# Expert weights in three pairs of buffers, activation rows in a ring of four, and the second gather moved to the end of GpSimd's step

## The chip, the cores and the metric

One core of one Trainium2 chip runs the whole kernel. The time is in device microseconds (us) for one execution; lower is better. Of the kernel before there are three timed runs and one profiled execution.

## The reference

One layer of a hybrid decoder for 520 tokens (512 prompt tokens and 8 new ones), width 1024, all in float32: attention and a recurrent branch side by side, a layer norm, then a mixture of experts and a second layer norm. The change touches only the last part:

```python
# 32 experts in 4 groups of 8; each token goes to the 2 best experts of its best group
for e in range(N_EXPERTS):
    gu = xt @ w_gate_up[e]                                # (n, 1024) @ (1024, 512)
    h = jax.nn.silu(gu[:, :D_EXPERT]) * gu[:, D_EXPERT:]
    y = y + gate[:, e:e + 1] * (h @ w_down[e])            # (n, 256) @ (256, 1024)
...
return _layernorm(ALPHA * x1 + ffn, ln2_g, ln2_b)
```

The weights of one expert are 3 MB (2 MB gate-up, 1 MB down), 96 MB in all. They are read from HBM once.

## The kernel before

The first part (about 340 us) computes attention, recurrence, output projection, first layer norm and the routing. The second part goes through the 32 experts in 16 pairs. A pair has 128 slots, 64 tokens for each of its two experts, and TensorE works on both experts side by side. Pair n is one *step*. Every token is in two slots, at an earlier and a later pair: the pair at which it comes first stores its expert's result in `first_rows` in HBM; the pair at which it comes second fetches that (the *partner's* rows), adds it, weighted, to its own, does the layer norm and stores the token's final row.

The order on each engine is written out by hand, with semaphores between engines. The first three pairs (HEAD) and the last five stand apart; eight (BODY) are in a loop that runs once here. In step n:

- **TensorE** (`products`, L970): gate-up product of pair n, in two halves of the weights (`gu_half`, `gu_ps`); then it turns the rows of pair n+1 (L955). Then `experts`: it waits for `h_ready` (VectorE), turns the hidden values, waits for their copy and does the down product (L993, `dn_ps`).
- **ScalarE**: silu (L1265), half of the turned rows' copy (L1253), the hidden values' copy (L1269), the copy of the down product to `yb` (L1276, `ya_done`), and `root(n-2)` (L1280) for the layer norm.
- **VectorE** (`pair_step`): `hidden(n)` (L1923, signals `h_ready`), `tokens_out(n+1)` (L1856), `residual(n+1)` (L1928, L1930), `finish(n-2)` (L1952 adds the partner's rows, then L1955 to L1969 are the layer norm), `own_part(n)` (L1944).
- **GpSimd** (Pool; indirect DMAs): `scatter_own(n)` (L2163, `yb` to `first_rows`), `scatter_out(n-2)` (L2180, the results), `gather_other(n)` (L2172, the partner's rows of pair n into `yo`), `gather_rows(n+4)` (L2150, input rows into `xg`).
- **SyncE** queues the weights (L413 gate-up, L416 down). There are six slots of 3 MB, one per expert. Pairs 0, 1 and 2 use slots 0/1, 2/3, 4/5; from pair 3 on only the first two pairs of slots are used in turn, since part of slots 4 and 5 holds rows: `xg` is a ring of eight. `refill(q, e, used)` waits for pair n-2's first half, second half and down product, and queues the matching parts of pair n behind each.

```python
S_XG = [5120, 6144, 0, D, S_RT] + [S_SLOT + D * n for n in range(3)]
S_YO = [S_SLOT + 3 * D, 2 * D, S_SLOT + 4 * D]
```

Of the kernel before, what the change touches and what calls it, by code (L numbers as in the profile page):

```python
# [8 lines left out]
ALU = mybir.AluOpType  # L9
# [7 lines left out]
P = 128  # L17
# [33 lines left out]
HEAD, BODY = 3, 8  # L51

# [43 lines left out]
S_XG = [5120, 6144, 0, D, S_RT] + [S_SLOT + D * n for n in range(3)]  # L96
S_YO = [S_SLOT + 3 * D, 2 * D, S_SLOT + 4 * D]
# [17 lines left out]
def nth(it, n, per=1, by=1, add=0):  # L115

    if isinstance(it, tuple):
        return it[0] * (by // per) + (n // per * by + add)
    v = n // per * by + add
    return v if it is None else it * (BODY // per * by) + v  # L120


def hymba_step(nc, xT, x_tok, kv_cache, rope_cache, conv_st, rec_st, page_rep, lane, w_in, w_kpe, w_uq, w_uk,
# [8 lines left out]
    with ExitStack() as ctx:  # L132
# [152 lines left out]
        yo_landed.append(sem("yo_landed2"))  # L285
# [52 lines left out]
        def ring(n):  # L338

            return n % BODY  # L340

        def other(it, n):

            return 2 if isinstance(it, tuple) and n == NPAIR - 1 else n % 2
# [16 lines left out]
        def _(sp):  # L361
# [89 lines left out]
            def refill(q, e, used):  # L451

                for half, done in enumerate((gu_half, gu_ps)):
                    sp.wait_ge(done, used)
                    for n in range(2):
                        gate_up(2 * q + n, slice(e + n, e + n + 1) if isinstance(e, int) else bass.ds(e + n, 1), half)
                sp.wait_ge(dn_ps, used)
                for n in range(2):
                    down(2 * q + n, slice(e + n, e + n + 1) if isinstance(e, int) else bass.ds(e + n, 1))
            refill(0, 6, 1)  # L460
            refill(1, 8, 2)
# [3 lines left out]
            with sp.Fori(0, n_rounds * (NE // 4) - 3) as it:  # L465
                refill(0, (it * 4 + 10) % NE, it * 2 + 4)
                refill(1, (it * 4 + 12) % NE, it * 2 + 5)
            refill(0, NE - 2, past + (NPAIR - 2))
# [14 lines left out]
        def _(pe):  # L483
# [475 lines left out]
            def products(it, n, last_pair=False):  # L959

                q, slots = n % 2, n if n < HEAD else (n - HEAD) % 2
                landed_count = 32 if n < HEAD else nth(it, n - HEAD, 2, 32, 64) if not isinstance(it, tuple) else \
                    it[0] * 16 + ((n - HEAD) // 2 * 32 + 64)
# [12 lines left out]
                if not last_pair:  # L976
                    turn_tokens(it, n + 1)
                return slots, landed_count
# [41 lines left out]
        def _(act):  # L1020
# [275 lines left out]
            for n in range(HEAD):  # L1296
# [8 lines left out]
                if n >= 2:  # L1305
                    root(None, n - 2)
            past = act.value_load(rounds[0:1, 1:2], min_val=0, max_val=(MAXR - 1) * NPAIR)
            with act.Fori(0, n_rounds * 2 - 1) as it:
                for n in range(HEAD, HEAD + BODY):
                    hidden(it, n)  # L1310
                    own_out(it, n)
                    root(it, n - 2)
# [6 lines left out]
            for n in range(HEAD + BODY, NPAIR - 1):  # L1319
                hidden((past,), n)  # L1320
                own_out((past,), n)
                root((past,), n - 2)
# [4 lines left out]
            root((past,), NPAIR - 3)  # L1327
            hidden((past,), NPAIR - 1, True)
            root((past,), NPAIR - 2)
# [4 lines left out]
        def _(dve):  # L1334
# [590 lines left out]
            def residual(it, n):  # L1925

                x = xg[ring(n)]
                stt(x, x, ALPHA, lng[:, 0, :], ALU.mult, ALU.mult).then_inc(residual_step, 1)  # L1928
                dve.wait_ge(residual_step, nth(it, n, 1, 2, 1))
                stt(x, lng[:, 1, :], ALPHA, x, ALU.mult, ALU.add).then_inc(residual_step, 1)  # L1930

            def own_part(it, n, last_pair=False):
# [4 lines left out]
                if last_pair:  # L1937
                    dve.wait_ge(dn_ps, nth(it, n, add=1))
                    y = ps[:, 5:7, :]
                    x = x.rearrange("p (a b) -> p a b", a=2)  # L1940
                else:
                    dve.wait_ge(ya_done, nth(it, n, add=1))
                    y = yb[n % 2]
                stt(x, y, g, x, ALU.mult, ALU.add).then_inc(own_added, 1)  # L1944

            def finish(it, n):

                x = xg[ring(n)]
                dve.wait_ge(own_added, nth(it, n, add=1))
                if n > 0:  # L1950
                    dve.wait_ge(yo_landed[other(it, n)], 16 if other(it, n) == 2 else nth(it, n + 1, 2, 16))
                    stt(x, yo[other(it, n)], known[:, n // QUAD % 2, 3, n % QUAD:n % QUAD + 1], x, ALU.mult, ALU.add).then_inc(finish_step, 1)  # L1952
                    dve.wait_ge(finish_step, nth(it, n, 1, 4, 1))
                    dve.wait_ge(mean_done, nth(it, n))
                first = V.bn_stats(bn[:, 0, :], x[:, 0:512])  # L1955
# [13 lines left out]
                stt(x, x, stat[:, 2:3], lng2[:, 1, :], ALU.mult, ALU.add).then_inc(out_ready, 1)  # L1969

            def pair_step(it, n):
# [5 lines left out]
                if n >= 2:  # L1977
                    finish(it, n - 2)
# [6 lines left out]
            landed(dve, ln1_landed, 3)  # L1985
            residual(None, 0)
# [8 lines left out]
            finish((past,), NPAIR - 3)  # L1995
            hidden((past,), NPAIR - 1)
            finish((past,), NPAIR - 2)
            own_part((past,), NPAIR - 1, True)
            finish((past,), NPAIR - 1)
# [3 lines left out]
        def _(pool):  # L2003
# [143 lines left out]

            def gather_rows(n, at):
# [3 lines left out]
                                     bounds_check=TOK - 1, oob_is_err=False).then_inc(gathered[n % 4], 16)  # L2152
# [5 lines left out]
            def scatter_own(it, n):  # L2158
# [5 lines left out]
                                     in_=yb[n % 2], in_offset=None, bounds_check=TOK - 1,  # L2164
                                     oob_is_err=False).then_inc(scattered[n % 2], 16)

            def gather_other(it, n):
                there, before = number(nth(it, n, QUAD, 16, 16), nth(it, n - 1, 2, 16, 16))
                fixed()
                pool.wait_ge(known_landed, there)  # L2170
# [158 lines left out]
```

## Time and profile before

| | |
|---|---|
| median of 3 runs | 599.1 us (598.02 to 601.4) |
| profiled execution, its own time | 599.66 us |
| its span in the profile | 598.0 us |
| granted TensorE clock, mean | 0.981 |
| busy: TensorE / VectorE / ScalarE / GpSimd | 87% / 62% / 32% / 23% |
| moved by DMA | 157.95 MB, mean 264 GB/s |

The span goes from the first to the last recorded work; the time is 1.7 us longer. TensorE's 87% is a mean over two parts: its busy share in the 40 slices is 9 tenths or more for most of the first half and 6 to 8 tenths in the last 150 us, where the DMA engines are at 9 tenths or more.

### The profile page before, as it was taken

The numbers are of one execution on the slowest core, as the hardware profiler recorded it, in microseconds if no ns is written. First come the engines' busy times: TensorE is split into PE (matmuls) and PEld (weight loads), VectorE is DVE, ScalarE is ACT, GpSimd is POOL, SyncE is SP. The second block draws the span as 40 slices with busy tenths as digits, with TensorE's granted clock in tenths as the row PEclk, the third lists the DMA queues.
The fourth block names the chain that finished last, engine by engine and source line by source line (L and its number), as shares of the span: only waits on it lengthen the run. The fifth ranks groups of instructions, "written<-read, shape, count | busy, mean of one in ns | idle before, by whom it ended". The sixth has DMA issues, their size and how long they took to land.

```text
span 598.0 us, 8961 instructions
## 1 busy us (share of the span) xinstructions
PE 519.1 (87%) x3296; PEld 280.1 (47%) x3296; DVE 372.9 (62%) x722; ACT 190.9 (32%) x356; POOL 134.7 (23%) x156
## 2 busy tenths in 40 slices
PE   6999999999988978999999798888887867867860
PEld 5887788874355533455456643333332222222220
DVE  0652059898935585643177766678885667666686
ACT  0100384213345552141132122444443334432340
POOL 1001054600028730000000202333323231221231
PEclk9999999999999999999899999999998989999996
DMA  8950008570709631003967599999999999999951
GB/s 308 379 178 6 1 1 348 212 256 1 282 3 361 272 145 56 2 35 137 424 225 304 190 417 412 405 394 418 416 416 409 421 415 418 416 414 418 403 205 41
DMA packets 34298, 157.95 MB, mean 264 GB/s; under 512 B 12712, under 2 KB 12712, under 8 KB 20304
## 3 DMA queue, kind: packets, MB, share of 16 engines
q1 hardware_dynamic: 20880, 127.46, 53.2%
q0 software_dynamic: 10752, 29.59, 13.1%
q10 hardware_dynamic: 2624, 0.34, 0.4%
q8 instruction: 26, 0.43, 0.3%
q14 instruction: 16, 0.13, 0.1%
HBM read 160.12 MB, written 21.23 MB: 303 GB/s over the span
## 4 chain that ended last, share of the span: by engine, by line
PE 60%; DMA 23%; ACT 7%; DVE 6%; issue 3%; SPq 1%; POOL 0%; POOLq 0%; ACTq 0%; DVEq 0%
DMA arena_o<-in_w_gu 19%; PE ps L496 17%; PE ps L970 11%; PE ps L756 9%; PE ps L993 4%; PE ps L597 3%; PE ps L659 2%; PE ps L643 2%; ACT arena_s L1253 2%; PE ps L680 2%; PE ps L955 1%; DMA x_rows<-arena_s 1%; PE ps L563 1%; PE ps L819 1%; DMA arena_s<-first_rows,known 1%
## 5 line engine op out<-in xcount | busy, mean ns | idle before, releaser
L970 PE MATMUL ps<-arena_w,arena_s 128*64 128x512 f32 x368 | 110.9, 606 | 22.3 <-DMA arena_o<-in_w_gu 10.9
L496 PE MATMUL ps<-arena_w 128*128 128x260 f32 x416 | 95.0, 389 | 5.2 <-DMA arena_w<-in_xT 4.7
L496 PEld LDWEIGHTS ps<-arena_w 128*128 128x128 f32 x416 | 79.8, 193 | 19.9 <-DMA arena_w<-in_xT 5.4
L970 PEld LDWEIGHTS ps<-arena_w,arena_s 128*64 128x64 f32 x368 | 33.5, 139 | 96.3 <-issue 68.8
L993 PE MATMUL ps<-arena_w,cs 128*64 128x512 f32 x184 | 54.8, 599 | 20.8 <-ACT cs L1269 20.8
L756 PE MATMUL ps<-arena_o,arena_s 128*128 128x512 f32 x128 | 61.6, 629 | 1.6 <-DVE arena_s L1614 1.6
L970 PE MATMUL ps<-arena_o,arena_s 128*64 128x512 f32 x112 | 53.6, 629 | 0.0
L1486 DVE STREAM_TRANSPOSE arena_s<-arena_w 128x1024 f32<-128x1024 f32 x36 | 42.0, 1215 | 8.3 <-PE ps L597 8.2
L2163 POOL DMA_INDIRECT first_rows<-arena_s,known x15 | 18.0, 1202 | 113.7 <-ACT arena_s L1276 104.8
L1923 DVE TENSOR_TENSOR arena_s<-arena_s,ps 128x256 f32<-128x256 f32 x16 | 6.7, 420 | 55.8 <-ACT arena_s L1265 55.8
L756 PEld LDWEIGHTS ps<-arena_o,arena_s 128*128 128x128 f32 x128 | 24.5, 201 | 33.4 <-issue 33.3
L993 PEld LDWEIGHTS ps<-arena_w,cs 128*64 128x64 f32 x184 | 15.9, 137 | 49.7 <-issue 29.1
L2150 POOL DMA_INDIRECT arena_s<-x_rows,arena_s x7 | 8.0, 1140 | 121.3 <-DMA x_rows<-arena_s 116.9
L1276 ACT COPY arena_s<-ps 128x1024 f32<-128x1024 f32 x15 | 15.2, 1012 | 57.7 <-PE ps L993 57.7
L1614 DVE SCALAR_TENSOR_TENSOR arena_s<-ps,rinv,arena_s 128x512 f32<-128x512 f32 x16 | 11.9, 747 | 32.6 <-PE ps L756 32.5
L1253 ACT ACTIVATE arena_s<-ps,vec 128x128 f32<-128x128 f32 x64 | 24.0, 456 | 14.4 <-PE ps L955 14.4
L1265 ACT ACTIVATE arena_s<-ps 128x256 f32<-128x256 f32 x16 | 6.1, 383 | 70.0 <-PE ps L970 69.9
L659 PE MATMUL ps<-arena_s 96*128 96x512 f32 (+3 forms) x64 | 24.1, 460 | 3.2 <-ACT arena_s L1125 2.9
L2180 POOL DMA_INDIRECT out_y<-arena_s,known x16 | 18.4, 1148 | 36.6 <-DVE arena_s L1969 36.3
L1125 ACT ACTIVATE arena_s<-ps,nm 128x512 f32<-128x512 f32 (+3 forms) x32 | 16.9, 528 | 29.5 <-DVE nm L1494 28.9
L1494 DVE TENSOR_REDUCE nm<-ps 128x1 f32<-128x512 f32 (+3 forms) x32 | 15.2, 482 | 17.0 <-PE ps L661 16.6
L993 PE MATMUL ps<-arena_o,cs 128*64 128x512 f32 x56 | 25.5, 599 | 0.0
(349 smaller groups left out, 893.1 us busy)
## 6 DMA issues: line engine op xcount, KB each, us to landing
arena_w<-in_w_gu SPq DMA_DIRECT2D x46, 1024.0 KB, 20.1
arena_w<-in_w_dn SPq DMA_DIRECT2D x23, 1024.0 KB, 20.2
arena_o<-in_w_gu SPq DMA_DIRECT2D x14, 1024.0 KB, 23.4
arena_o<-in_w_dn SPq DMA_DIRECT2D x7, 1024.0 KB, 23.8
arena_w<-in_w_in SPq DMA_DIRECT2D x12, 512.0 KB, 13.1
arena_o<-in_w_out SPq DMA_DIRECT2D x1, 4096.0 KB, 13.8
arena_s<-in_w_gu SPq DMA_DIRECT2D x4, 1024.0 KB, 8.1
first_rows<-in_x_tok SPq DMA_DIRECT2D x1, 2080.0 KB, 18.5
```

The source lines that it names most:

```text
L496: last = mm(ps[rows, b + n, 0:HALF], lhs(k), rhs(k)[:, n * HALF:(n + 1) * HALF], start=(k == 0), stop=(k == ks - 1))
L597: last = mm(ps[32 * i:32 * i + NH, r, :], qs[32 * r:32 * r + 32, SB * b + i, c, :], T[n % 2][32 * r:32 * r + 32, i, :], start=(c == 0), st ...
L659: mm(ps[:, b, 0:P * (i + 1)], qh[0:96, h, i * P:(i + 1) * P], kh[0:96, h, 0:P * (i + 1)], start=True, stop=False)
L756: last = mm(ps[:, 4 + w, :], (attT if w == 0 else recT)[:, k, t * P:(t + 1) * P], wo[:, KR * w + k, n * 512:(n + 1) * 512], start=(k == 0) ...
L970: last = mm(ps[64 * e:64 * e + 64, 2 + q, :], xgT[:, k, CAP * e:CAP * (e + 1)], gu_w[2 * slots + e][:, k, :], start=(k == 0), stop=(k == K ...
L993: last = mm(ps[64 * e:64 * e + 64, 5 + h, :], hT[:, f, CAP * e:CAP * (e + 1)], dn_w[2 * slots + e][:, f, h * 512:(h + 1) * 512], start=(f ...
L1125: fn(Pb[h % 2][:, OFF[i]:OFF[i] + P * (i + 1)], ps[:, 4 + n % 2, 0:P * (i + 1)], ACT.Exp, bias=nm[:, h % 2, i:i + 1], accum_out=lsum[:, h ...
L1253: last = fn(xgT[:, k, :], ps[:, k // 4, (k % 4) * P:(k % 4 + 1) * P], ACT.Identity, bias=vec[:, V_LB + k:V_LB + k + 1], scale=vec[:, V_LG ...
L1276: nc.scalar.copy(yb[n % 2].rearrange("p (a b) -> p a b", a=2), ps[:, 5:7, :]).then_inc(ya_done, 1)
L1486: last = V.transpose(T[n % 2][:, u, :].rearrange("p s (j x) -> p s j x", j=16), src)
L2163: G.indirect_dma_start(out=first_rows, out_offset=bass.IndirectOffsetOnAxis(ap=place(0, n), axis=0), in_=yb[n % 2], in_offset=None, bounds ...
L2180: G.indirect_dma_start(out=y_out, out_offset=bass.IndirectOffsetOnAxis(ap=place(1, n), axis=0), in_=xg[ring(n)], in_offset=None, bounds_ch ...
```

## The change

Five things change together.

1. **Rows.** The ring of `xg` has four tiles instead of eight. `finish` writes its result to `yo[n % 2]`, which held the partner's rows, and not back to `xg`. `finish(n-1)`, `root(n-1)` and `scatter_out(n-1)` stand in step n, where `n-2` stood. `residual` uses norm parameters that are multiplied by ALPHA once.
2. **GpSimd's step.** It is `scatter_own(n)`, `scatter_out(n-1)`, `gather_rows(n+3)`, `gather_other(n)`. The bound of the indirect DMAs comes from a register that is set once.
3. **Weights.** Slots 4/5 are free of rows, and pairs go to the three pairs of slots by a table. A pair's weights are queued when the pair that last used its slots is done: three pairs back for most, two for pairs 8 and 9.
4. **Slot 4.** Its gate-up weights (pair 2) are queued right behind the last store of `x1_rows`, and only its down weights wait for that store and for the first gather.
5. **The last pair.** VectorE adds the partner's rows ahead of the wait for the down product; `finish(14)` stands ahead of `hidden(15)`; TensorE does five small products before that wait.

```diff
+BUFFER = (0, 1, 2, 0, 1, 0, 1, 2)
-S_XG = [5120, 6144, 0, D, S_RT] + [S_SLOT + D * n for n in range(3)]
-S_YO = [S_SLOT + 3 * D, 2 * D, S_SLOT + 4 * D]
+S_XG = [5120, 6144, 0, D]
+S_YO = [S_RT, 2 * D]
...
+def pair_buffer(n):
+
+    return n if n < HEAD else BUFFER[(n - HEAD) % BODY]
...
         def ring(n):
 
-            return n % BODY
+            return n % 4
...
             store_x1(4)
+            for half in range(2):
+                gate_up(4, slice(4, 5), half)
             landed(sp, x1_stored, TT)
             landed(sp, gathered[0])
-            for half in range(2):
-                gate_up(4, slice(4, 5), half)
             down(4, slice(4, 5))
...
             def finish(it, n, last_pair=False):
...
-                stt(x, x, stat[:, 2:3], lng2[:, 1, :], ALU.mult, ALU.add).then_inc(out_ready, 1)
+                stt(yo[n % 2], x, stat[:, 2:3], lng2[:, 1, :], ALU.mult, ALU.add).then_inc(out_ready, 1)
 
             def pair_step(it, n):
                 hidden(it, n)
...
-                if n >= 2:
-                    finish(it, n - 2)
+                if n >= 1:
+                    finish(it, n - 1)
                 own_part(it, n)
...
             def pair_step(it, n):
 
                 scatter_own(it, n)
-                if n >= 3:
-                    outs, = number(nth(it, n - 2, 1, 16))
-                    fixed()
-                    pool.wait_ge(out_landed, outs)
-                if n >= 2:
-                    scatter_out(it, n - 2)
                 if n >= 1:
+                    scatter_out(it, n - 1)
+                    m = n + 3
...
+                        gather_rows(m, rows_at.bitcast(I32)[:, m // QUAD % 2, m % QUAD:m % QUAD + 1])
                     gather_other(it, n)
```

GpSimd's instructions in one step of the loop, before: the store of pair n's own results, the store of the finished rows of pair n-2, the gather of the partner's rows of pair n, the gather of the input rows of pair n+4.

```order
L2163 DMA first_rows<-arena_s,known 520x1024 [waits ya_done,known_landed,routed]
L2145 ISA
L2145 ISA [waits out_landed,routed]
L2180 DMA out_y<-arena_s,known 520x1024 [waits out_ready,routed]
L2145 ISA
L2172 DMA arena_s<-first_rows,known 128x1024 [waits scattered1,known_landed,routed]
L2150 DMA arena_s<-x_rows,rows_at 128x1024 [waits rows_at_landed,routed]
L2145 ISA
```

The same step in the changed kernel, where the finished rows are those of pair n-1 and the input rows those of pair n+3:

```order
L2190 DMA first_rows<-arena_s,known 520x1024 [waits ya_done,known_landed,routed]
L2169 ISA
L2212 DMA out_y<-arena_s,known 520x1024 [waits out_ready,out_landed,routed]
L2177 DMA arena_s<-x_rows,rows_at 128x1024 [waits rows_at_landed,routed]
L2169 ISA
L2201 DMA arena_s<-first_rows,known 128x1024 [waits out_landed,scattered1,known_landed,routed]
L2169 ISA
```

The gather of the partner's rows (into `arena_s` from `first_rows`) has moved behind the gather of the input rows, and the store ahead of both now waits for the `out_ready` of pair n-1.

VectorE at the end of the program, before: `hidden(15)` and all of `finish(14)`; `own_part(15)`, which waits for `dn_ps`, comes next.

```order
L1923 TENSOR_TENSOR arena_s<-arena_s,ps 128x256 [waits silu_done]
L1952 SCALAR_TENSOR_TENSOR arena_s<-arena_s,known 128x1024 [waits yo_landed0,own_added]
L1953 REGISTER_ALU
L1955 BN_STATS bn<-arena_s 128x6 [waits mean_done,finish_step]
L1958 BN_STATS bn<-arena_s 128x6
L1959 REGISTER_ALU
L1962 MEMSET stat 128x1 [waits out_ready,finish_step]
L1963 BN_AGGR stat<-bn 128x2
L1965 SCALAR_TENSOR_TENSOR arena_s<-arena_s,stat,arena_o 128x1024 [waits mean_done]
L1967 RECIPROCAL stat<-stat 128x1 [waits root_done]
L1968 REGISTER_ALU
L1969 SCALAR_TENSOR_TENSOR arena_s<-arena_s,stat,arena_o 128x1024 [waits finish_step]
```

In the changed kernel, from the end of `finish(14)` over `hidden(15)` to the beginning of the last layer norm:

```order
L1994 SCALAR_TENSOR_TENSOR arena_s<-arena_s,stat,arena_o 128x1024 [waits finish_step]
L1946 TENSOR_TENSOR arena_s<-arena_s,ps 128x256 [waits silu_done]
L1967 REGISTER_ALU
L1971 REGISTER_ALU [waits residual_step]
L1972 SCALAR_TENSOR_TENSOR arena_s<-arena_s,known 128x1024 [waits yo_landed1]
L1973 REGISTER_ALU
L1978 SCALAR_TENSOR_TENSOR arena_s<-ps,known,arena_s 128x1024 [waits dn_ps,mean_done,finish_step]
L1980 BN_STATS bn<-arena_s 128x6 [waits own_added]
```

`hidden(15)` (the 128x256 product) has moved behind the whole of `finish(14)`, and the partner's rows of pair 15 are added ahead of the instruction that waits for `dn_ps`.

SyncE around the last store of `x1_rows`, before: the slots 3 and 4 and the store between them.

```order
L413 DMA arena_o<-in_w_gu 128x2048 [waits o_done]
L413 DMA arena_o<-in_w_gu 128x2048
L416 DMA arena_o<-in_w_dn 128x2048
L421 DMA x_rows<-arena_s 128x1024 [waits ln_norm]
L413 DMA arena_s<-in_w_gu 128x2048 [waits gathered0,x1_stored]
L413 DMA arena_s<-in_w_gu 128x2048
L416 DMA arena_s<-in_w_dn 128x2048
```

And in the changed kernel:

```order
L433 DMA arena_o<-in_w_gu 128x2048 [waits o_done]
L433 DMA arena_o<-in_w_gu 128x2048
L436 DMA arena_o<-in_w_dn 128x2048
L441 DMA x_rows<-arena_s 128x1024 [waits ln_norm]
L433 DMA arena_s<-in_w_gu 128x2048 x2
L436 DMA arena_s<-in_w_dn 128x2048 [waits gathered0,x1_stored]
```

The two gate-up transfers of slot 4 no longer carry the wait for `gathered0` and `x1_stored`; the down transfer does.

## Rows read from the trace of the kernel before

**Rows 1.** The page: busy share of the DMA engines, 40 slices
```profile
DMA  8950008570709631003967599999999999999951
```

**Rows 2.** DMA view, 400 to 560 us: queues; issues, count, median us to landing
```profile
DMA packets 14696, 66.43 MB, mean 415 GB/s; under 512 B 5833, under 2 KB 5833, under 8 KB 7364
...
q1 hardware_dynamic: 8235, 59.99, 90.2%
q0 software_dynamic: 5731, 6.29, 11.2%
...
out_y<-arena_s,known POOLq DMA_INDIRECT x11, 8.2
arena_s<-first_rows,known POOLq DMA_INDIRECT x11, 9.7
...
arena_s<-x_rows,rows_at POOLq DMA_INDIRECT x9, 11.9
```

**Rows 3.** Chain that ended last, 395 to 424 us: start us, us, what
```profile
396.33 6.87 PE ps L970 x32
...
406.08 3.65 PE ps L993 x16
409.73 6.87 PE ps L970 x32
```

**Rows 4.** Groups by line, 400 to 560 us: busy us, mean ns, idle before
```profile
L970 PE MATMUL ps<-arena_w,arena_s 128*64 128x512 f32 x244 | 77.3, 611 | 18.6 <-DMA arena_o<-in_w_gu 10.9 <-DMA arena_w<-in_w_gu 7.6
```

**Rows 5.** Timeline, 545 to 560 us: start us, us, engine, line, operation
```profile
550.25 1.28 DVE L1952 SCALAR_TENSOR_TENSOR arena_s<-arena_s,known 128x1024 f32<-128x1024 f32 x1
...
554.94 1.29 DVE L1969 SCALAR_TENSOR_TENSOR arena_s<-arena_s,stat,arena_o 128x1024 f32<-128x1024 f32 x1
...
557.09 1.20 POOL L2180 DMA_INDIRECT out_y<-arena_s,known  x1 [1.80 <-DVE arena_s L1969]
```

**Rows 6.** Timeline of Pool, 469 to 479 us
```profile
472.68 1.18 POOL L2180 DMA_INDIRECT out_y<-arena_s,known  x1 [1.94 <-DVE arena_s L1969]
474.16 1.04 POOL L2172 DMA_INDIRECT arena_s<-first_rows,known  x1 [0.30 <-issue]
475.50 1.01 POOL L2150 DMA_INDIRECT arena_s<-x_rows,rows_at  x1 [0.30 <-issue]
```

**Rows 7.** DMA view, 334 to 340 us: the four first gathers
```profile
arena_s<-x_rows,arena_s POOLq DMA_INDIRECT x4, 4.1
```

**Rows 8.** Chain that ended last, 325 to 342 us
```profile
326.92 7.77 DMA x_rows<-arena_s
...
335.48 4.18 DMA arena_s<-x_rows,arena_s
```

**Rows 9.** Timeline of Pool, 340 to 380 us
```profile
369.51 1.26 POOL L2163 DMA_INDIRECT first_rows<-arena_s,known  x1 [8.34 <-DMA known<-slot_table]
...
378.92 1.86 POOL L2172 DMA_INDIRECT arena_s<-first_rows,known  x1 [4.74 <-DMA first_rows<-arena_s,known]
```

**Rows 10.** Stretches: us, busy us (x) of each engine, PEclk, DMA share, GB/s
```profile
334.00:340.00 6.00, 5.15 (x47) 4.96 (x46) 3.94 (x22) 0.29 (x2) 3.61 (x4) 1.00 0.31 87
...
530.00:550.00 20.00, 13.95 (x66) 4.86 (x68) 13.78 (x22) 7.41 (x15) 3.40 (x3) 1.00 1.02 417
570.00:580.00 10.00, 6.77 (x31) 1.94 (x28) 9.15 (x13) 3.21 (x5) 4.07 (x4) 1.00 0.51 198
```

**Rows 11.** Timeline of the end, 578 to 598 us: VectorE and TensorE
```profile
579.37 0.41 DVE L1923 TENSOR_TENSOR arena_s<-arena_s,ps 128x256 f32<-128x256 f32 x1
...
580.74 3.65 PE L993 MATMUL ps<-arena_w,cs 128*64 128x512 f32 x16 [0.46 <-ACT cs L1269]
581.15 1.28 DVE L1952 SCALAR_TENSOR_TENSOR arena_s<-arena_s,known 128x1024 f32<-128x1024 f32 x1 [1.36 <-DMA arena_s<-first_rows,known]
...
585.43 1.28 DVE L1969 SCALAR_TENSOR_TENSOR arena_s<-arena_s,stat,arena_o 128x1024 f32<-128x1024 f32 x1
...
589.27 0.69 DVE L1955 BATCH_NORM_STATS2 bn<-arena_s 128x6 f32<-128x512 f32 x1
```

More of the change, by code:

```diff
@@ L120, in nth, with before_in, weights_landed @@
     return v if it is None else it * (BODY // per * by) + v
+def pair_buffer(n):
+    return n if n < HEAD else BUFFER[(n - HEAD) % BODY]
+def before_in(n):
+    d = 1
+    while BUFFER[(n - HEAD - d) % BODY] != pair_buffer(n):
+        d += 1
+    return d
+def weights_landed(it, n):
+    if n < HEAD:
+        return 32
+    m, q = n - HEAD, pair_buffer(n)
+    per = BUFFER.count(q)
+    v = 32 * (2 + m // BODY * per + BUFFER[:m % BODY].count(q))
+    return it[0] * (4 * per) + v if isinstance(it, tuple) else it * (32 * per) + v
 def hymba_step(nc, xT, x_tok, kv_cache, rope_cache, conv_st, rec_st, page_rep, lane, w_in, w_kpe, w_uq, w_uk,
@@ L464, in _ @@
             past = sp.value_load(rounds[0:1, 1:2], min_val=0, max_val=(MAXR - 1) * NPAIR)
[L465 to L468, printed above, removed]
+            with sp.Fori(0, n_rounds * 2 - 1) as it:
+                for n in range(HEAD + 2, HEAD + 2 + BODY):
+                    refill(it, n)
+            for n in range(HEAD + 2 + BODY, NPAIR):
+                refill((past,), n)
             landed(sp, outs_stored, 6)
@@ L977, in products @@
                     turn_tokens(it, n + 1)
+                else:
+                    for _ in range(5):
+                        mm(ps[:, 7, 0:P], ident[:, :], ident[:, :], start=True, stop=True)
                 return slots, landed_count
@@ L1311, in _ @@
                     own_out(it, n)
-                    root(it, n - 2)
+                    root(it, n - 1)
                     if n % QUAD == QUAD - 1:
@@ L1321, in _ @@
                 own_out((past,), n)
-                root((past,), n - 2)
+                root((past,), n - 1)
                 if n % QUAD == QUAD - 1:
@@ L1994, in _ @@
                 pair_step((past,), n)
-            finish((past,), NPAIR - 3)
+            finish((past,), NPAIR - 2)
             hidden((past,), NPAIR - 1)
-            finish((past,), NPAIR - 2)
-            own_part((past,), NPAIR - 1, True)
-            finish((past,), NPAIR - 1)
+            finish((past,), NPAIR - 1, True)
         @block.gpsimd
@@ L2228, in _ @@
                 pair_step((past,), n)
-            n = NPAIR - 1
-            gather_other((past,), n)
-            for k in range(3):
-                scatter_out((past,), n - 2 + k)
-            fixed()
-            landed(pool, out_landed, n_rounds * NPAIR)
+            gather_other((past,), NPAIR - 1)
+            scatter_out((past,), NPAIR - 2)
+            ready, before, stored = number(nth((past,), NPAIR - 1, add=1), nth((past,), NPAIR - 1, 1, 16), n_rounds * (16 * NPAIR))
+            scatter_out((past,), NPAIR - 1, ready, before)
+            pool.wait_ge(out_landed, stored)
 def _lay_out(i):
```

100 lines of the change are left out of this document (52 added, 48 removed).

## The prediction

> **What bounds the kernel now.** I read the page first, for where the DMA engines are full: in its last third, from slice 24 to slice 38 of 40, their row shows nines [rows 1]. So the expert part is the one to look at, and for it the DMA view: from 400 to 560 us all queues together move 415 GB/s, of which the weights' queue q1 moves 59.99 MB, 375 GB/s, and the rows' queue q0 only 6.29 MB [rows 2]. A pair's weights are 6.29 MB, so 16.8 us at that pace. The chain of waits shows what TensorE alone would need: gate-up of two following pairs starts at 396.33 and 409.73 us, 13.4 us apart, with no wait for a DMA between [rows 3]. In the groups by line TensorE waits 18.6 us for weights between 400 and 560 us [rows 4]. The picture: the first pairs after 342 us run at 13.4 us from what is in the slots, the later ones at the pace of the weights, and the queue of weights is never empty in between. A third pair of buffers cannot make a full queue faster. What can be won there is an earlier start of the stream (the DMA share is only 0.31 from 334 to 340 us, [rows 10]) and a shorter end.
>
> Next I read what a pair's finish hangs on. In the timeline the add of the partner's rows starts at 550.25, the layer norm's last instruction at 554.94, and the store of these rows on GpSimd at 557.09 [rows 5]: 6.84 us from the partner's rows to the store. GpSimd then issues one indirect DMA after the other: store 472.68, second at 474.16, third at 475.50, so the third starts 2.82 us behind the first [rows 6]. From its issue the first lands after 8.2 us, the second after 9.7, the third after 11.9 (medians) while weights flow [rows 2]; on idle DMA engines the four first gathers land after 4.1 us [rows 7].
>
> **The new loop.** Before, the partner's gather of pair n is issued behind the store of pair n-2 and needed in step n+2: gather, finish, store, next gather takes 6.84 + 1.48 + 9.7 = 18.0 us and has two steps (26.8 us at least) to run in. It never holds anything. The change puts the finish one step behind instead of two and the gather third. Now: partner's rows of n-1 landed, `finish(n-1)`, `out_ready`, store of n-1, rows gather, partner's gather of n, and that one is what `finish(n)` waits for in the next step. This is one closed lap for each pair, and no engine can run ahead of it: on VectorE `own_part(n)` and `hidden(n+1)` are queued behind `finish(n-1)`, and TensorE's down product waits for `hidden`; on ScalarE the next silu is behind `root`; on GpSimd all gathers and `scatter_own(n+1)` are behind the store; SyncE's refills wait for TensorE's counters. A lap is
>
> - with weights flowing: 6.84 + 2.82 + 11.9 = 21.6 us;
> - on idle DMA engines: 6.84 + 2.82 + 4.1 = 13.8 us;
>
> against 13.4 us of TensorE and 16.8 us of weights. That the third place costs what the input gather paid there (11.9) is my choice; the bounds are 4.1 and 11.9. The register for the bound saves at most the 0.3 us gaps between issues [rows 6]; I count nothing.
>
> **Start.** The routing table arrives at 369.5 us (the store of pair 0's own results ends its wait then, [rows 9]). `own_part(0)` and `finish(0)` take about 6 us, so the first store goes at about 375.5, the input gather at 377, the partner's gather of pair 1 at about 378.5 (in the kernel before, it also waits for the stored own results and starts at 378.92, [rows 9]). It lands some 11.5 us later, at 390. Slot 4's gate-up weights, 2.1 MB or 5 us, now lie in the queue at 327.3. The last store of `x1_rows` was issued at 326.92 and took 7.77 us, the first gather 4.18 us [rows 8]; the store is ahead of the new transfers in its queue, the gathers compete with them. Bounds 0 and 11.9 - 4.1 = 7.8 us; since 2.1 MB are gone by about 339, I take 2 us. The table is made after pair 0's first product, so this shifts everything: F(1), the start of `finish(1)`, is at 392.
>
> **Laps.** Thirteen laps lead from F(1) to F(14). The refills get the queue from about 349 us, behind the 3.1 MB of slot 4 and norm parameters that wait for the first gather (340 us). By 392 16 MB of them are through (43 us at 375 GB/s), 2.6 of 13 pairs; 10.4 pairs or 65.6 MB are left, 175 us of a full queue. If only full and idle laps existed: 175 / 21.6 = 8.1 full ones and 4.9 idle ones, 175 + 68 = 243 us, 18.7 on average. But a lap longer than 16.8 us leaves gaps in the stream, and one falls where the gather lies: the down weights of a slot are only queued after a down product, about 13 us behind F(n) (6.9 us to the end of `finish` and `own_part`, then 0.4, 1.0 and 3.65), and by then a backlog of one gate-up load is drained. Walking the laps singly, the queue runs dry around pairs 5 to 7 (pair 8's weights wait for pair 6, and pair 10's, which pair 5 sets free, are queued behind pair 9's, which wait for pair 7) and after pair 15's weights: 21, 18, 15, 19, 18, 21, 21, 20, 20, 19, 15, 13.4, 13.4 = 234 us. F(14) is then 626, by the two-state sum 635. I take 628.
>
> **End.** `hidden(15)` now stands behind `finish(14)`. From the rows of the end [rows 11]: 581.15 to the end of the last norm instruction 5.56 us, `hidden` 0.41, from there to the down product 0.96 (it ended at 579.78 and the product started at 580.74), the product 3.65, adding it 1.3 (the same form takes 1.28 us, [rows 5]), and from the first norm statistic at 589.27 to the end of the span 8.76: 20.7 us. In the kernel before F(14) is 581.15 and the end 16.9 us later, so the end is 3.8 us longer from there, though an instruction is saved.
>
> **Sum** against the profiled execution (599.66 us for a span of 598.0, 0.1% above the median of 599.1): 392 + 236 + 20.7 + 1.7 = 650 us, +8.5%. The early weights are worth 5 us only if the weights bound; the five small products of the last pair lie in the wait for `hidden(15)`; `residual` is as long as before; the scaling of the norm parameters, 2048 columns against the 1024 of a 1.28 us instruction [rows 5], is about 2.6 us on VectorE, once, ahead of `own_part(0)`, which waits for the routing table anyway. These count nothing; without that cover they would be 2.6 us together with under 1 us of products.
>
> **A page that says otherwise.** The Trainium skill, page "DMA: Bandwidth & Descriptors", section "Anatomy of one DMA — SWDGE (gpsimd) path", fits a GpSimd DMA as about 2.0 us plus bytes at 436 GB/s. An estimate by it for 128 rows of 4 KB is 3.2 us, the lap would be 12.9 us, below TensorE's 13.4, and the loop would hold nothing: the first rival's case. On idle engines the trace is near it (4.1 us, [rows 7]), under weights it is not (8.2 to 11.9, [rows 2]).
>
> **Rivals.**
>
> - *The loop is hidden, the stream of weights bounds still, faster.* For it: idle landings of 4.1 us. The stream starts 5 us earlier, and with it `hidden(15)`, 579.37 us now [rows 11]: 574.4 + 0.41 + 0.96 + 3.65 + 1.3 + 8.76 = 589.4, plus 1.7 is 591 us. It needs a mean lap of (599.7 - 22.4 - 392) / 13 = 14.25 us just to reach no change, a mean landing of 4.6 us. Against it: 11 landings in second place have a median of 9.7 us. Chance 0.08, and 0.02 for a landing right at that point.
> - *The loop binds, but the gathers mostly meet gaps.* Landings of 5.5 to 7 us, laps 15.2 to 16.7: 392 + 198 to 217 + 22.4 = 612 to 632 us, most likely 622. For it: the walk above has such laps at pair 3. Against it: weights of 10 pairs need 175 us at any rate. Chance 0.16.
> - *The loop binds with a full queue to the end, or TensorE's clock falls in its longer waits.* All laps 21.6: 392 + 281 + 22.4 = 695 us. The granted clock is 1.00 even from 570 to 580 us with TensorE 68% busy [rows 10], and a lap of 18 us leaves it 74% busy, so I see no reason for the clock. Chance 0.06.
> - *The forecast*, laps of 16.7 to 19.8 us, 632 to 672 us: 0.68.
>
> **Numbers.** 612 to 672 us holds 0.84 of the chance. A measurement of this kernel tells about 0.5% from no change. Faster by more than that 0.08, within 0.02, slower 0.90.
>
> **What would show it.** Right: VectorE's add of the partner's rows waits for DMA `first_rows` in nearly each step (one wait of 1.4 us now), ScalarE's or TensorE's waits move from weights to `h_ready`, laps are uniform between stores on GpSimd, the DMA share falls clearly below 1.0 between 430 and 580 us, and almost no product waits for weights. The partner's gather lands after 6 to 12 us. Wrong: the DMA share stays at 1.0 until 570 us, the stores follow each other at 13 to 17 us, and the landings of the third gather are under 5 us. What could make it wrong is above all the share of q1 and q0 when both are full, which sets the landing.

## The result: 646.7 us, and the profile after

Each kernel was timed in turn with the kernel before on the same chip. The changed kernel takes 646.7 us (median of 4 runs, 643.27 to 648.76), the kernel before 599.8 us (4 runs, 598.02 to 601.4). The ratio is 1.078, with a 95% interval of 1.074 to 1.082: 47 us slower. The profiled execution is the slowest of the four (648.8 us) and has a span of 646.8 us and a mean granted clock of 0.928, against 598.0 us and 0.981.

The page of the changed kernel, in 40 slices of 16.2 us, TensorE's granted clock and the DMA engines:

```profile
PEclk9999999999999899999989996897979689777987
DMA  8930035904176310068799999972989999994110
```

In the expert part, from slice 22 on, the DMA row still has its nines, with one gap at slice 28 (437 to 453 us), and it stays full to slice 36, which ends at 582 us; [rows 1] stays full to slice 38, which ends at 568 us. The weights are done later than before, and then another 65 us pass. The clock row has sixes, sevens and eights in the expert part.

The waits between 340 and 650 us: the engine, its instruction, what it waited for, us in total, times, longest.

```profile
POOL out_y L2212 <- DVE arena_s L1994: 135.0, 16, 13.4
DVE arena_s L1972 <- DMA arena_s<-first_rows,known: 104.0, 13, 11.0
ACT stat L1304 <- DVE stat L1988: 96.0, 15, 10.4
...
PE ps L1008 <- DVE arena_s L1946: 72.7, 11, 9.2
```

These rows are one wait seen from four engines. VectorE's add of the partner's rows (L1972) waits 104.0 us for the gather; one wait of 1.36 us is seen in [rows 11]. The store on GpSimd waits for the layer norm behind that add, ScalarE for its root, and TensorE for `hidden`, which VectorE does after `finish`. Now one lap, between two stores of finished rows:

```profile
552.23 1.24 POOL L2212 DMA_INDIRECT out_y<-arena_s,known  x1 [10.61 <-DVE arena_s L1994]
...
553.78 1.04 POOL L2177 DMA_INDIRECT arena_s<-x_rows,rows_at  x1 [0.31 <-issue]
...
555.12 1.10 POOL L2201 DMA_INDIRECT arena_s<-first_rows,known  x1 [0.30 <-issue]
...
561.05 1.02 POOL L2190 DMA_INDIRECT first_rows<-arena_s,known  x1 [4.83 <-ACT arena_s L1300]
...
566.32 1.28 DVE L1972 SCALAR_TENSOR_TENSOR arena_s<-arena_s,known 128x1024 f32<-128x1024 f32 x1 [9.73 <-DMA arena_s<-first_rows,known]
...
570.69 1.28 DVE L1994 SCALAR_TENSOR_TENSOR arena_s<-arena_s,stat,arena_o 128x1024 f32<-128x1024 f32 x1
...
572.81 1.24 POOL L2212 DMA_INDIRECT out_y<-arena_s,known  x1 [10.73 <-DVE arena_s L1994]
```

Read it from the top. The store of the finished rows is issued at 552.23, the gather of the input rows at 553.78 and the gather of the next pair's partner rows at 555.12. The add that needs these rows starts at 566.32, 11.2 us later. The norm's last instruction is at 570.69, and the next store at 572.81. A lap is 20.6 us: 2.9 us of issues on GpSimd, 11.2 us of landing, and 6.5 us from the add to the next store. The store of own results (561.05) lies inside and holds nothing. The chain that ended last has the same picture: between 380 and 600 us, 51.4% of it is the landing of `first_rows`.

The DMA view from 400 to 560 us, to be laid beside [rows 2]:

```profile
DMA packets 12555, 57.68 MB, mean 361 GB/s; under 512 B 4890, under 2 KB 4890, under 8 KB 6157
...
q1 hardware_dynamic: 7188, 52.33, 79.7%
...
arena_s<-first_rows,known POOLq DMA_INDIRECT x9, 11.9
```

In these 160 us the weights' queue moved 52.33 MB, where it had moved 59.99. The nine gathers of partner rows had a median landing of 11.9 us. The same in stretches (us, busy us and instructions of PE, PEld, DVE, ACT, POOL, then granted clock, DMA share, GB/s):

```profile
334.00:340.00 6.00, 5.35 (x49) 5.17 (x48) 3.93 (x23) 0.43 (x2) 4.07 (x4) 1.00 0.83 297
340.00:347.00 7.00, 5.36 (x30) 2.49 (x29) 5.80 (x23) 1.51 (x4) 0.00 (x0) 1.00 0.91 315
430.00:450.00 20.00, 12.80 (x58) 4.49 (x56) 14.44 (x22) 7.09 (x12) 4.40 (x4) 0.83 0.25 89
490.00:570.00 80.00, 52.27 (x230) 18.55 (x230) 38.09 (x58) 20.89 (x34) 16.35 (x15) 0.85 1.02 417
...
590.00:610.00 20.00, 14.02 (x62) 5.11 (x64) 16.69 (x26) 9.51 (x18) 6.67 (x6) 0.83 0.17 49
```

The DMA engines are busy from slot 4's early weights (0.83 at 334 to 340 us, 0.31 in [rows 10]), empty for three quarters of 430 to 450 us, full again from 490 to 570 us, and done by 590 us. From there on TensorE has all weights, and it still waits 8.12 us for `hidden(15)`, as the timeline of the end shows further down.

### The profile page after: what moved, and what is told of

Its sections match the earlier page's. It is cut to its first block, busy times and chain, and to the rows that moved or that the text cites. A ratio compares the mean times of both kernels' runs of the same rounds, so it can differ in the third digit from the quotient of the medians.

```text
span 646.8 us, 8877 instructions
## 1 busy us (share of the span) xinstructions
PE 533.2 (82%) x3306; PEld 285.6 (44%) x3306; DVE 372.3 (58%) x723; ACT 193.7 (30%) x358; POOL 136.1 (21%) x156
## 4 chain that ended last, share of the span: by engine, by line
PE 48%; DMA 22%; DVE 13%; issue 8%; ACT 6%; POOL 3%; POOLq 0%; DVEq 0%; SPq 0%; ACTq 0%
DMA arena_s<-first_rows,known 18%; PE ps L519 16%; PE ps L779 8%; PE ps L1017 3%; PE ps L991 3%; PE ps L620 3%; DVE arena_s L1994 3%; DVE arena_s L1972 2%; PE ps L666 2%; PE ps L682 2%; POOL arena_s L2177 2%; DVE arena_s L1990 1%; PE ps L703 1%; DMA first_rows<-arena_s,known 1%; DVE bn L1983 1%
## 5 line engine op out<-in xcount | busy, mean ns | idle before, releaser
L519 PEld LDWEIGHTS ps<-arena_w 128*128 128x128 f32 x416 | 80.2, 194 | 20.5 <-DMA arena_w<-in_xT 5.6
L991 PE MATMUL ps<-arena_w,arena_s 128*64 128x512 f32 x288 | 84.4, 592 | 1.6 <-DVE arena_s L1879 1.6
L1972 DVE SCALAR_TENSOR_TENSOR arena_s<-arena_s,known 128x1024 f32<-128x1024 f32 x15 | 19.2, 1283 | 104.0 <-DMA arena_s<-first_rows,known 104.0
L1008 PE MATMUL ps<-ident,arena_s 128*128 128x128 f32 x32 | 9.5, 392 | 72.7 <-DVE arena_s L1946 72.7
L991 PEld LDWEIGHTS ps<-arena_w,arena_s 128*64 128x64 f32 x288 | 27.1, 137 | 56.0 <-issue 54.1
L991 PE MATMUL ps<-arena_o,arena_s 128*64 128x512 f32 x96 | 42.2, 592 | 0.0
L1008 PEld LDWEIGHTS ps<-ident,arena_s 128*128 128x128 f32 x32 | 4.1, 180 | 76.0 <-DVE arena_s L1946 75.9
L1304 ACT ACTIVATE stat<-stat,eps 128x1 f32<-128x1 f32 x16 | 4.7, 294 | 96.1 <-DVE stat L1988 96.0
L2177 POOL DMA_INDIRECT arena_s<-x_rows,arena_s x6 | 6.2, 1028 | 116.7 <-DMA x_rows<-arena_s 115.2
L1637 DVE SCALAR_TENSOR_TENSOR arena_s<-ps,rinv,arena_s 128x512 f32<-128x512 f32 x16 | 11.9, 747 | 31.0 <-PE ps L779 30.9
L1017 PE MATMUL ps<-arena_o,cs 128*64 128x512 f32 x48 | 29.5, 769 | 0.0
L991 PE MATMUL ps<-arena_s 128*64 128x512 f32 x128 | 28.1, 592 | 0.0
## 6 DMA issues: line engine op xcount, KB each, us to landing
arena_o<-in_w_gu SPq DMA_DIRECT2D x12, 1024.0 KB, 14.4
arena_w<-in_w_in SPq DMA_DIRECT2D x12, 512.0 KB, 13.3
```

Of the source, the lines that this page charges most:

```text
L519: last = mm(ps[rows, b + n, 0:HALF], lhs(k), rhs(k)[:, n * HALF:(n + 1) * HALF], start=(k == 0), stop=(k == ks - 1))
L991: last = mm(ps[64 * e:64 * e + 64, 2 + q, :], xgT[:, k, CAP * e:CAP * (e + 1)], gu_w[2 * slots + e][:, k, :], start=(k == 0), stop=(k == K ...
L1017: last = mm(ps[64 * e:64 * e + 64, 5 + h, :], hT[:, f, CAP * e:CAP * (e + 1)], dn_w[2 * slots + e][:, f, h * 512:(h + 1) * 512], start=(f ...
L1972: stt(x, yo[n % 2], known[:, n // QUAD % 2, 3, n % QUAD:n % QUAD + 1], x, ALU.mult, ALU.add).then_inc(finish_step, 1)
L2177: G.indirect_dma_start(out=xg[ring(n)], out_offset=None, in_=x1_rows, in_offset=bass.IndirectOffsetOnAxis(ap=at, axis=0), bounds_check=lim ...
```

## The experiments

The first five test the loop. Small differences between experiments are best taken from the ratios, since the kernel before took 599.4, 600.1 and 598.8 us beside them. `F(n)` is the start of `finish(n)`, the add of the partner's rows, as in the prediction.

**e1, the partner's gather first.** The loop is opened: GpSimd issues it ahead of the store that waits for `finish(n-1)`.

```diff
+                if n >= 1:
+                    gather_other(it, n)
                 scatter_own(it, n)
...
                         gather_rows(m, ...)
-                    gather_other(it, n)
```

> The changed kernel, with the partner's gather of pair n issued first in GpSimd's step n, ahead of both stores; it then no longer stands behind out_ready of pair n-1. My theory (the closed lap of finish, store and third gather holds every step): the lap is open, so the laps fall to the pace of weights and TensorE, 13.4 to 17 us, the queue of weights is full again from 350 to 565 us, and the time is 588 to 603 us, most likely 594, below the kernel before. Rival A (the third pair of buffers and its table leave the queue of weights dry, and that is the loss): the weights' table is the same, so 635 to 650 us. Rival B (TensorE's lower granted clock in its waits is the loss): a clock of 0.83 and over 630 us if the clock is a cause; if the clock only follows from waits, it goes back to over 0.95.

Measured: 604.3 us, ratio 1.008 (1.005 to 1.011). Of 47 us, 42 are back. VectorE's wait for the partner's rows fell from 104.0 to 19.2 us, and the mean granted clock went from 0.928 back to 0.970, as it should if the clock follows the waits (rival B). It is not the kernel before again, and another wait stands at the top:

```profile
POOL arena_s L2201 <- DMA out_y<-arena_s,known: 129.3, 14, 11.1
```

GpSimd's timeline between 499 and 531 us says why (the wait before an instruction is in brackets):

```profile
499.83 1.00 POOL L2212 DMA_INDIRECT out_y<-arena_s,known  x1 [0.30 <-issue]
501.14 1.03 POOL L2177 DMA_INDIRECT arena_s<-x_rows,rows_at  x1 [0.31 <-issue]
511.10 1.63 POOL L2201 DMA_INDIRECT arena_s<-first_rows,known  x1 [8.93 <-DMA out_y<-arena_s,known]
513.03 1.02 POOL L2190 DMA_INDIRECT first_rows<-arena_s,known  x1 [0.30 <-issue]
514.35 1.00 POOL L2212 DMA_INDIRECT out_y<-arena_s,known  x1 [0.30 <-issue]
515.66 1.04 POOL L2177 DMA_INDIRECT arena_s<-x_rows,rows_at  x1 [0.31 <-issue]
526.97 1.01 POOL L2201 DMA_INDIRECT arena_s<-first_rows,known  x1 [10.27 <-DMA out_y<-arena_s,known]
```

The partner's gather (L2201) writes into the tile of `yo` that the results two pairs back were stored from, so it waits until that store has landed. The store is third in a burst of four. From its issue to the gather that waits for it pass 11.3 us (499.83 to 511.10) and 12.6 us (514.35 to 526.97), and the burst repeats about every 15 us. F(1) to F(14) take 192.6 us, 14.8 a pair, against 186.7 us or 14.4 a pair in the kernel before. Between 380 and 600 us the landing of this store is 40.9% of the chain that ended last, and the landing of the input rows' gather, fourth in the burst, 12.7%. One more wait belongs to this order: TensorE waits once, 8.4 us, for the input rows of pair 4.

**e2, the partner's gather second**, behind the store and ahead of the input rows: the loop stays closed, one place shorter.

> The changed kernel, with the partner's gather second (behind the store, ahead of the input gather) instead of third. My theory: the lap stays closed, but each loaded lap loses one issue of 1.34 us and the transfer of one gather ahead of it, 2 to 3 us: about 3.5 us in 9 loaded laps and little in the idle ones, so 612 to 628 us, most likely 618. Rivals A and B (the loss is in the weights' table or the clock): 642 to 649 us.

Measured: 628.3 us, ratio 1.047 (1.045 to 1.050). 18 us come back for one place, less than the most likely 618 us, and just outside the range of 612 to 628. F(1) to F(14) take 214.3 us, 16.5 a pair, and VectorE still waits 83.6 us. The long laps are about 3 us shorter, as expected: 16.6 to 19.0 us where they were 20.3 to 21.8. But there are ten of them instead of eight: two laps that were short in the changed kernel (14.7 and 13.2 us) take 19.0 and 17.6 us here. I had not counted that.

**e5, light weights.** The refills move one eighth of the columns of each weight tile; the other seven eighths are left out, and TensorE works on what lies in the slots. Everything else is as in the changed kernel.

> The changed kernel, but every refill of weights from pair 3 on moves an eighth of its columns; the rest of the weights in the slot are old ones, so the results are not the layer's. All instructions and waits are there. My theory: the lap is long because the third gather lands late while weights flow; on nearly idle DMA engines it lands after 4 to 5 us, laps are 13.4 to 14.5 us, and the time is 580 to 595 us, most likely 586. Rival D (the lap is long by fixed costs of GpSimd's issue order, whatever the load): laps of 18 us and over 630 us.

Measured: 580.6 us, ratio 0.966 (0.963 to 0.970). The landing of the partner's gathers, first in the changed kernel, then with light weights (shortest, median, longest):

```profile
DMA to landing us min/median/max: 3.1/11.1/12.5
```

```profile
DMA to landing us min/median/max: 2.9/3.6/4.4
```

The loop is still closed here, with the same order on every engine, and costs nearly nothing: VectorE waits 9.0 us for these rows, and F(1) to F(14) take 173.1 us, 13.3 a pair, which is TensorE's own pace of 13.4. So neither the order alone nor the weights alone cost 47 us. The lap is slow because its gather shares the DMA engines with a full queue of weights. The 580.6 us themselves are not a gain over the kernel before, which moves all its weights; that one was not run with light weights.

**e4, two pairs of buffers** instead of three, `BUFFER = (0, 1, 0, 1, 0, 1, 0, 1)`.

> The changed kernel with only two pairs of buffers in turn from pair 3 on, as before. My theory: the lap binds, not the weights; a refill two laps ahead (36 us or more) is early enough for 16.8 us of transfer, so 642 to 655 us, most likely 647, with little waiting for weights. Rival C (the third pair is worth something here and hides part of the loss): over 660 us. Rival A (the table of three is the loss): under 620 us.

Measured: 644.8 us, ratio 1.077 (1.074 to 1.080). The intervals overlap, so the third pair of buffers shows neither a gain nor a cost while the loop binds. The laps differ all the same: long ones of 19.8 to 22.4 us alternate with short ones of 13.9 to 16.0, the median landing is 5.5 us, and F(1) to F(14) take 227.4 us against 232.9. A median landing does not tell the mean lap where landings are of two kinds.

**e6, the kernel before with the partner's gather in third place.** Its finish is two steps behind, so the loop has two steps to run in.

```diff
-                if n >= 1:
-                    gather_other(it, n)
...
                     gather_rows(n + 4, ...)
+                if n >= 1:
+                    gather_other(it, n)
```

> The kernel before with only the order of the two gathers exchanged in GpSimd's step: input rows ahead, the partner's third, as in the change. My theory: place costs only where the lap is closed over one step; here the finish comes two steps behind, 6.84 + 2.82 + 11.9 = 21.6 us against two steps of at least 26.8 us, so no change, 597 to 602 us. Rival E (the third place by itself delays the finish): slower, over 610 us.

Measured: 600.1 us, ratio 1.000 (0.996 to 1.003). With e2 above it shows that the third place costs where the loop closes over one step, and not in the kernel before.

**a7 and b1, the end order**: `hidden(15)` ahead of `finish(14)` on VectorE, and its ScalarE part ahead of `root(14)`. First alone in the changed kernel (a7):

```diff
-            finish((past,), NPAIR - 2)
             hidden((past,), NPAIR - 1)
+            finish((past,), NPAIR - 2)
```

> The changed kernel with hidden(15) back ahead of finish(14) and nothing else. The end from the start of finish(14) took 23.1 us there, 16.9 us in the kernel before. If my sum is right in treating the end as a term of its own, 5 to 7 us less than 646.7: 640 to 642 us. Rival (the last step is held by the partner's rows as the others are): 645 to 648 us.

Measured: 638.8 us, ratio 1.065 (1.061 to 1.070), 7.9 us below the changed kernel's 646.7 and just below the range of 640 to 642. From F(14) to the end of the span it is 16.9 us instead of 23.1; these 6.2 us are the part that the edit explains. The laps take 227.9 us here for 232.9, with the same order in them, so the remaining 2 us are no effect of the edit that a row shows. Then on top of e1 (b1):

> The kernel with the partner's gather first, and hidden(15) put back ahead of finish(14) on VectorE and ScalarE. The end of the changed kernel took 23.1 us from the start of finish(14), with the last down product waiting for it; with the product beside finish(14) it should be 16.9 us as in the kernel before. So about 6 us less than the 604.3 us of the partner-first kernel: 596 to 600 us, most likely 598. Rival (the end hangs on the partner's rows of pair 15, not on the product): 602 to 605 us.

Measured: 599.9 us, ratio 1.001 (0.998 to 1.004), in the range, 4 us below e1. Against the kernel before, the profiled e1 has F(1) 7.4 us earlier (387.02 for 394.46), laps 5.9 us longer and an end 6.0 us longer (22.9 for 16.9); the end is what b1 works on, and its own is 18.6 us.

**a8 and e3, slot 4's weights.** Queued late again in the changed kernel (a8, the diff), and queued early in the kernel before (e3, the same edit the other way):

```diff
             store_x1(4)
-            for half in range(2):
-                gate_up(4, slice(4, 5), half)
             landed(sp, x1_stored, TT)
             landed(sp, gathered[0])
+            for half in range(2):
+                gate_up(4, slice(4, 5), half)
```

> The changed kernel with slot 4's gate-up weights back behind the first gather, as before. Where the lap binds, an earlier start of the weights is worth nothing: 645 to 650 us. Rival (the early start is worth its 5 us of stream here too): 650 to 653 us.

Measured: 649.2 us, ratio 1.084 (1.079 to 1.090), whose interval overlaps the changed kernel's.

> The kernel before with one part of the change alone: slot 4's gate-up weights queued right behind the last store. If the stream of weights sets the time of the kernel before, its start moves by up to 5 us and the end with it: 593 to 597 us, most likely 595. In the changed kernel the first gathers and TensorE's first expert product were not later than before, so no loss is expected. Rival: the gathers compete with the 2.1 MB and land later, which takes the gain back: 598 to 601 us.

Measured: 597.9 us, ratio 0.998 (0.996 to 1.001): a miss of the range of 593 to 597, and not told from no change. The rival's reason does not hold either: the first gate-up product starts at 341.82 us, no later than before (342.44). One stretch of the kernel before and then of this one:

```profile
370.00:390.00 20.00, 18.50 (x91) 6.64 (x88) 10.76 (x16) 6.76 (x12) 9.32 (x8) 1.00 1.00 407
```

```profile
370.00:390.00 20.00, 18.49 (x94) 6.95 (x90) 11.18 (x17) 6.41 (x11) 8.32 (x8) 1.00 0.83 316
```

The stream that started earlier ran dry here (DMA share 0.83 for 1.00): the next refill waits for a product, and is queued at 385.94 us where it was 386.55. An early start of a stream is kept only as far as its buffers reach, and most of the 5 us became this gap.

**b2, b3 and b4, making the third pair of buffers pay.** All stand on b1. The first, b2, is a table with a distance of three wherever possible, `BUFFER = (0, 1, 2, 0, 1, 2, 0, 1)`:

> The former with another table of buffers, 0 1 2 0 1 2 0 1, so that pair 8 refills what pair 5 has left instead of waiting for pair 6. In the partner-first kernel the queue of weights ran dry for about 8 us near 435 us. If the stream sets the time from there on, 3 to 6 us less than the former: 591 to 597 us, most likely 594. Rival (GpSimd's chain of stores, 14.8 us a step, or a gap that only moves to pair 11, sets the time): 596 to 600 us, no difference.

Measured: 602.1 us, ratio 1.004 (1.001 to 1.006), a miss. The dry stretch moved from 430 to 450 us (DMA share 0.74 in b1, 0.61 in e1) to 470 to 490 us (0.76). TensorE's gate-up products wait for no weights any more (5.8 us in b1), but its wait for input rows grew from 13.2 to 17.8 us, and GpSimd's wait for the landing of the store stayed: 134.1 us in 14 times. The second, b3, stores the results ahead of the own results, so that they stand second in the burst:

```diff
+                if n >= 2:
                     gather_other(it, n)
+                    scatter_out(it, n - 1)
                 scatter_own(it, n)
```

> As the end-order kernel, with GpSimd's step from pair 2 on: partner's gather, store of the finished rows, store of the own results, input gather; step 1 keeps the order of the changed kernel, so that the rows of pair 4 are not late. Two losses of the end-order kernel should go: the 8 us that TensorE waited for the rows of pair 4, and the chain of GpSimd's stores (partner, own, result store, its landing) of about 15 us a step, which becomes about 12.5 us. Then weights or TensorE (13.4 us) set the pace: 589 to 596 us, most likely 592. Rival (the weights' stream with its dry spell near 435 us is the bound already): 597 to 601 us, no gain.

Measured: 602.1 us, ratio 1.006 (1.004 to 1.008), a miss too. The top row of its waits:

```profile
POOL arena_s L2201 <- DMA first_rows<-arena_s,known: 91.0, 11, 10.8
```

The gather now waits for the own results of the step before, which have gone to third place in their turn. It needs both stores, and one of them is always third: F(1) to F(14) take 192.3 us, 14.8 a pair. TensorE's wait for the input rows of pair 4 is gone (0.2 us for 8.4), and nothing is gained by it. The landings of this burst in its order, from 400 to 560 us, medians:

```profile
arena_s<-first_rows,known POOLq DMA_INDIRECT x10, 7.9
out_y<-arena_s,known POOLq DMA_INDIRECT x10, 9.4
first_rows<-arena_s,known POOLq DMA_INDIRECT x10, 11.4
arena_s<-x_rows,rows_at POOLq DMA_INDIRECT x10, 13.4
```

b4 is both edits together:

> The same with the table 0 1 2 0 1 2 0 1. With GpSimd's chain out of the way the stream's dry spell is what is left; with this table pair 8's weights are queued at pair 5. 588 to 595 us, and 0 to 4 us below the former. Rival (the spell only moves to pair 11, whose weights now wait for pair 9): the same as the former or 1 to 3 us above it.

Measured: 602.2 us, ratio 1.003 (1.001 to 1.006), the same again.

## Why the prediction was right

By its own steps:

- **The loop** is what happened, in the places named: VectorE waits for `first_rows` 13 times, the other waits are `h_ready` and `out_ready`, and no row of TensorE's waits between 340 and 650 us names the weights. The largest group of the gate-up product:

```profile
L991 PE MATMUL ps<-arena_w,arena_s 128*64 128x512 f32 x288 | 84.4, 592 | 1.6 <-DVE arena_s L1879 1.6
```

Opening the loop (e1) gives 42 of 47 us back, and thinning out the queue of weights (e5) makes the same loop harmless.

- **A full lap** was put at 21.6 us. The eight long laps took 20.3 to 21.8, with landings up to 12.5 us. In the lap shown above the three terms are 6.5, 2.9 and 11.2 us for 6.84, 2.82 and 11.9. The landing of 11.9 for the third place was a choice between bounds of 4.1 and 11.9 with nothing behind it but one row; it came out (median 11.9 from 400 to 560 us, 11.1 over all).
- **Thirteen laps** took 232.9 us (F(1) at 390.81, F(14) at 623.74), predicted 236. The walk was 21, 18, 15, 19, 18, 21, 21, 20, 20, 19, 15, 13.4, 13.4; the laps were 21.2, 21.0, 13.0, 21.4, 14.7, 21.8, 21.6, 20.3, 20.5, 20.6, 13.2, 11.5, 12.1. The laps of 13.0 and 14.7 come where the walk had 15 and 18, and all short ones are shorter than it had; two laps that it had at 18 and 19 were long (21.0 and 21.4). The shortest landing was 3.1 us. Against the kernel before (F(1) 394.46, F(14) 581.15, 186.7 us) the start is 3.7 us earlier, the laps are 46.2 us longer and the end 6.2 us: the loss lies in the laps.
- **The start**: F(1) was put 1.2 us too late, at 392 for 390.8. The 2 us for gathers delayed by slot 4's early weights were not paid, though the four gathers did land later, after 9.3 us (median) for the 4.1 of [rows 7]: the product of pair 0 needs only the first of them, which landed after 4.30 us for the 4.18 of [rows 8]. The turn of the first rows starts at 339.69 us and the first gate-up product at 342.43, as before (342.44). The partner's gather of pair 1 went later than I had it, at 380.19 for 378.5, since it waited 1.5 us longer for the stored own results, and landed after 10.5 us for 11.5.
- **The end** was put at 20.7 us and took 23.1. Here a term was mis-sized, the down product of pair 15, put at 3.65 us. The timeline from the five small products on:

```profile
620.19 1.38 PE L1001 MATMUL ps<-ident 128*128 128x128 f32 x10
...
623.74 1.28 DVE L1972 SCALAR_TENSOR_TENSOR arena_s<-arena_s,known 128x1024 f32<-128x1024 f32 x1 [4.84 <-DMA arena_s<-first_rows,known]
...
629.22 0.41 DVE L1946 TENSOR_TENSOR arena_s<-arena_s,ps 128x256 f32<-128x256 f32 x1
...
629.69 0.69 PE L1008 MATMUL ps<-ident,arena_s 128*128 128x128 f32 x2 [8.12 <-DVE arena_s L1946]
...
630.84 1.11 PE L1017 MATMUL ps<-arena_w,cs 128*64 128x512 f32 x1 [0.46 <-ACT cs L1293]
...
634.31 0.99 PE L1017 MATMUL ps<-arena_w,cs 128*64 128x512 f32 x1
...
635.14 0.59 PE L1017 MATMUL ps<-arena_w,cs 128*64 128x512 f32 x1
...
636.00 0.59 PE L1017 MATMUL ps<-arena_w,cs 128*64 128x512 f32 x1
...
636.74 1.28 DVE L1978 SCALAR_TENSOR_TENSOR arena_s<-ps,known,arena_s 128x1024 f32<-128x1024 f32 x1 [5.91 <-PE ps L1017]
```

The small products stand at the start of TensorE's wait and are over at 621.57 (620.19 and 1.38 us); the 8.12 us for `hidden(15)` come behind them. The down product starts at 630.84 with matmuls of 1.11 us and only at the end has its usual 0.59. It takes 5.8 us, to 636.6. Where the end order is turned back in the changed kernel (a7), the wait is not there, and the product's matmuls take 0.59 to 0.64 us throughout.

- **The clock** I had wrong as a statement. The rival said TensorE's clock might fall in its longer waits, and I saw no reason for it. It did fall: 0.83 to 0.85 in the laps against 1.00 in [rows 10]. In the long laps TensorE still waits 6.5 to 9.2 us for `hidden` each time, so the slower down products (4.8 us and more for 3.65) are covered there; at the end they are not and cost about 2 us. The rival as a whole, full queue to the end, did not happen.
- **DMA share**: "clearly below 1.0 between 430 and 580 us" was only partly right. It was 0.25 at 430 to 450 us, but 1.02 from 490 to 570 us. My walk had seen this, my sentence on what would show it had not: a queue can be full for a long stretch and the stream still be late overall.
- **Slot 4 and the buffers** were counted as nothing while the loop binds; a8 and e4 bear it out.

The sum, 650.4 us before rounding, stands against a profiled execution of 648.8: -1.2 at the start, -3.1 in the laps (F(14) at 623.7 for 628), +2.4 at the end, and +0.3 between span and time. That the total is so near is in part luck: errors of 4 and 3 us cancel, and the 236 us of the laps were set between two counts of 234 and 243. The 5 us by which a7 and the changed kernel differ in their laps, with the same order, say how well such a sum can be known.

The Trainium skill, page "DMA: Bandwidth & Descriptors", section "Anatomy of one DMA — SWDGE (gpsimd) path", fits such a DMA as about 2.0 us plus its bytes at 436 GB/s, by which the estimate was 3.2 us. The light weights come near it (median 3.6 us); beside a full queue of weights the median is 11.1 us, and the measurement decides.

What stays open is what the third pair of buffers is worth when nothing on GpSimd holds the step. With the loop open, GpSimd's chain of a burst and the wait for its third landing, 15 us a pair, took its place; that rests on the waits and on the chain that ended last (the store's landing is 40.9% of it in e1 and 63.4% in b1, between 380 and 600 us), not on an experiment that removes it. A third tile of `yo` would break that chain; it was not tried, and whether there is room for it was not settled. It might bring little, for the fourth landing is behind it: in b2 the input rows' gather is 25.6% of the chain, beside 26.5% for the store. No version that moves all weights is clearly faster than the kernel before.

## What to carry to other kernels

Before an order is shortened by one step to save buffers, follow each value round: if a store waits for a result that needs a gather queued behind the store of the step before, the step is at least the sum of that lap, and the gather's landing must be taken from a row with the queues as full as they will be then (here 3.6 or 11.1 us, median, for the same 512 KB). Then look at what comes second: a buffer that is read by a store and rewritten by a gather makes the store's landing part of the step too. And a stream that was started earlier brought only what the free buffers held here: the refill behind them waited for a product that had hardly moved.

## What the runs showed of the hardware

- The landing of an indirect DMA of 128 rows of 4 KB beside a full queue of weights depends on its place in the burst: 7.9, 9.4, 11.4 and 13.4 us (medians) for the first to the fourth in b3, gathers and stores alike, at a DMA share of 1.02 from 450 to 560 us. In e1 and in b3 the chain was set by whichever store stood third. The partner's gather landed 11.1 us (median) after its issue with full weights and 3.6 us with light ones.
- TensorE's granted clock was 0.83 to 0.85 on average from 490 to 590 us in the changed kernel, with TensorE busy 65% of the time from 490 to 570 us and waits of 6.5 to 9.2 us ended by `hidden`. Right after such a wait the matmuls of 512 columns took 1.06 to 1.11 us (the 1.2 GHz level), later 0.59 us (2.4 GHz). In the kernel before TensorE is busy 70% of 530 to 550 us, in waits of 1.8 us at most, and the clock was 1.00 [rows 10]. The five small products of the last pair stand ahead of such a wait and left 8.12 us of it. What decides between the two levels was not tried.
